# Low parts of the smaller weight tiles of the attention stages subtracted by GpSimd in place of VectorE, in a four-layer transformer kernel on one core

## What is computed

```python
# block 1, per layer                     # block 2, per layer
x = x + 0.5*swiglu(rmsnorm(x), ...)      h = adaln(rms_norm(x), shift1, scale1)
h = rmsnorm(x)                           proj = h @ w_in            # q, k, v, gates
q, k, v, ..., gates = h @ w_in           y_a = swa_attention(...)  @ w_o_swa
y_a = forgetting_attention(...)          y_b = moba_attention(...) @ w_o_moba
y_b = stick_breaking_attention(...)      mixed = sigmoid(gate_a)*y_a + sigmoid(gate_b)*y_b
y_c = dsa_attention(...)  # top-k mask   x = x + gt1 * (mixed @ w_out)
merged = sum(sigmoid(gates)*(y @ w_up))  h = adaln(rms_norm(x), shift2, scale2)
x = x + merged @ w_out                   x = x + gt2 * (relu(h @ w_up)**2 @ w_down)
x = x + 0.5*swiglu(rmsnorm(x), ...)
```

## Time and profile before

| what | value |
|---|---|
| median of 3 runs | 2033.84 us (2031.59 to 2033.9) |
| the profiled execution: its time, its span | 2032.25 us, 2030.6 us |
| granted TensorE clock, mean over the span | 0.996 |
| busy PE, share of the span | 1960.0 us, 97% |
| busy DVE | 1526.7 us, 75%, 2637 instructions |
| busy ACT | 1031.0 us, 51% |
| busy POOL | 44.9 us, 2%, 80 instructions |
| the chain that ended last | PE 82%, DVE 9%, ACT 6%, issue 3%, DMA 1% |

### The profile page before, as it was taken

One profiled execution on the slowest core, in us unless ns is written; L12 is line 12 of the kernel. 1 busy time (PEld: TensorE's weight loads), 2 busy tenths in 40 slices (PEclk: granted clock), 3 DMA queues, 4 the chain that ended last, 5 costly groups with the idle time before them and its releaser, 6 DMA issues.

```text
span 2030.6 us, 32702 instructions
## 1 busy us (share of the span) xinstructions
PE 1960.0 (97%) x11980; PEld 1718.1 (85%) x11980; DVE 1526.7 (75%) x2637; ACT 1031.0 (51%) x1582; POOL 44.9 (2%) x80
## 2 busy tenths in 40 slices
PE   7999999999999999999899999999999999999998
PEld 6888898988888888899888888888788888887887
DVE  7887567579888987657678887785767778667766
ACT  5445545654446444545565445566444455555443
POOL 0000000000000000000000000000000000000000
PEclk9999999999999999999999999999999999999999
DMA  7874543257774876453246774441455544233553
GB/s 298 293 283 172 190 156 131 88 180 280 277 268 153 287 281 215 167 186 125 94 169 247 282 250 150 170 149 71 145 186 186 186 179 173 95 125 135 186 186 135
DMA packets 77286, 382.18 MB, mean 188 GB/s; under 512 B 9296, under 2 KB 9472, under 8 KB 55936
## 3 DMA queue, kind: packets, MB, share of 16 engines
q1 hardware_dynamic: 67392, 329.78, 44.9%
q0 software_dynamic: 9792, 51.00, 7.6%
HBM read 379.65 MB, written 1.10 MB: 188 GB/s over the span
## 4 chain that ended last, share of the span: by engine, by line
PE 82%; DVE 9%; ACT 6%; issue 3%; DMA 1%; SPq 0%; DVEq 0%; ACTq 0%
PE psum L674 21%; PE psum L585 15%; PE psum L586 15%; PE psum L587 15%; PE psum L677 11%; DVE weights_low_a L1446 2%; ACT weights_high_a L1069 1%; PE psum L883 1%; ACT x_normed L1077 1%; PE psum L821 1%; PE psum L812 1%; PE psum L910 1%; PE psum L911 1%; PE psum L909 1%; DMA raw_a<-in_w_ffn_a_a 1%
## 5 line engine op out<-in xcount | busy, mean ns | idle before, releaser
L674 PE MATMUL psum<-h_high_low,weights_high_a 128*128 128x512 f32 x1840 | 654.7, 398 | 5.4 <-DVE h_high_low L1491 3.3
L1446 DVE TENSOR_TENSOR weights_low_a<-raw_a,weights_high_a 128x2048 fp32r<-128x2048 f32 (+1 forms) x232 | 459.8, 1983 | 123.2 <-ACT weights_high_a L1069 121.2
L677 PE MATMUL psum<-h_high_low,weights_low_a 128*128 128x256 f32 x1840 | 514.2, 279 | 0.0
L674 PEld LDWEIGHTS psum<-h_high_low,weights_high_a 128*128 128x128 f32 x1840 | 345.3, 188 | 92.5 <-issue 5.3
L1069 ACT ACTIVATE weights_high_a<-raw_a 128x2048 fp32r<-128x2048 f32 (+1 forms) x232 | 386.0, 1664 | 65.1 <-PE psum L587 61.4
L677 PEld LDWEIGHTS psum<-h_high_low,weights_low_a 128*128 128x128 f32 x1840 | 346.7, 188 | 6.6 <-issue 1.0
L1446 DVE TENSOR_TENSOR weights_low_b<-raw_b,weights_high_b 128x1024 fp32r<-128x1024 f32 x224 | 273.3, 1220 | 54.5 <-ACT weights_high_b L1069 54.0
L1069 ACT ACTIVATE weights_high_b<-raw_b 128x1024 fp32r<-128x1024 f32 x224 | 235.4, 1052 | 104.6 <-PE psum L587 104.6
L1139 ACT ACTIVATE up_low_products<-psum 128x512 f32<-128x512 f32 (+1 forms) x146 | 74.1, 507 | 391.7 <-PE psum L677 391.6
L585 PE MATMUL psum<-weights_high_b,gated_high 128*128 128x512 f32 x608 | 241.8, 398 | 4.6 <-DVE gated_low L1575 2.8
L587 PE MATMUL psum<-weights_high_b,gated_low 128*128 128x512 f32 x608 | 241.3, 397 | 0.0
(11 more groups left out here) (300 smaller groups left out, 3165.9 us busy)
## 6 DMA issues: line engine op xcount, KB each, us to landing
ada_weights<-in_w_ada POOLq DMA_DIRECT2D x64, 768.0 KB, 5.9
raw_a<-in_w_ffn_a_a SPq DMA_DIRECT2D x44, 1024.0 KB, 7.3
raw_a<-in_w_ffn_b_a SPq DMA_DIRECT2D x44, 1024.0 KB, 7.4
raw_a<-in_w_ffn_a SPq DMA_DIRECT2D x64, 512.0 KB, 4.4
raw_b<-in_w_ffn_b SPq DMA_DIRECT2D x64, 512.0 KB, 3.3
raw_a<-in_w_proj_a SPq DMA_DIRECT2D x28, 1024.0 KB, 5.5
raw_a<-in_w_gate_a SPq DMA_DIRECT2D x26, 1024.0 KB, 4.8
raw_b<-in_w_ffn_a_b SPq DMA_DIRECT2D x44, 512.0 KB, 3.9
```

The costliest lines, as they stand in the source:

```text
L674: pe.matmul(ps[:, bank, :], whi[0][:, p, c:c + P], hboth[:, k, :, :].rearrange("p a b -> p (a b)"), start=k == 0, stop=False, skip_group_c ...
L677: last_mm = pe.matmul(ps[:, bank, SEQ:2 * SEQ], wlo[0][:, p, c:c + P], hhi[:, k, :], start=False, stop=k == KD - 1, skip_group_check=True)
L1446: dve.tensor_tensor(wlo[kind][:, p, 0:width], raw[kind][:, p, 0:width], whi[kind][:, p, 0:width].bitcast(F32), ALU.subtract).then_inc(lo_r ...
```

## The change

In the attention stages the low parts of the "b" tiles are subtracted by GpSimd. DVE no longer does them there: 8 tiles per layer in block 1 (slots `FF1+9` to `FF1+16`) and 5 in block 2 (slots 7 to 12, of which slot 11 has no "b" tile), 26 in all. GpSimd waits for the low part of the slot before (so that `lo_ready[1]` still counts in order) and for ACT's high part. In `merge`, DVE waits for GpSimd's last tile before it goes on with its own. The "a" tiles and all splits outside the attention stages stay as they are.

```diff
+            def low_b_ready(l, blk, n):
+                slots = SL[blk]
+                return l * parts_before(slots, 1, len(slots)) + lo_before(blk, 1) + parts_before(slots, 1, n + 1) + 2
+
+            def split_low_b(l, blk, first, end):
+
+                for n in range(first, end):
+                    p, width = n % 2, SL[blk][n][1] * P
+                    if not width:
+                        continue
+                    pool.wait_ge(lo_ready[1], low_b_ready(l, blk, n - 1))
+                    pool.wait_ge(now().hi_ready[1], parts_before(SL[blk], 1, n + 1))
+                    pool.tensor_tensor(wlo[1][:, p, 0:width], raw[1][:, p, 0:width],
+                                       whi[1][:, p, 0:width].bitcast(F32), ALU.subtract).then_inc(lo_ready[1], 1)
...
+                if blk == 2:
+                    split_low_b(l, 2, 7, 13)
                 if blk == 1:
 
+                    split_low_b(l, 1, FF1 + 9, FF1 + 17)
                     pool.wait_ge(now().scale_ready, 2 * NT + 1)
...
-                    if g is not None and g % 3 == 0:
-                        split_low(l, blk, 1, n0 + g // 3 + 1)
...
                 split_low(l, blk, 0, n0 + 1)
+                dve.wait_ge(lo_ready[1], l * parts_before(SL[blk], 1, len(SL[blk])) + lo_before(blk, 1)
+                            + parts_before(SL[blk], 1, n0 + 1) + 2)
```

## The result

| | before | after |
|---|---|---|
| median of 4 runs each, us | 2033.13 | 2044.64 |
| profiled span, us | 2030.6 | 2042.2 |

The ratio is 1.0056, with an interval of 1.0044 to 1.0069: the change makes the kernel slower by about 11.5 us. The forecast was 2037.6 us with a range up to 2042.5. The sign had been given the larger chance (slower 0.41, faster 0.25); the size lies outside the range.

The account below looks back on a forecast made before the run. PE, busy 97%, bounds the kernel, so only its waits and slow stretches count. The places sum to +2.8 us, twice +5.6, less 1.85 for the clock: +3.8, 2037.6 us on the median, range 2026.5 to 2042.5.

Parts of the forecast that it names:

- The hold itself: A DVE instruction with two SBUF inputs stands still for the rest of a running GpSimd subtraction; forecast's chance 0.60.
- A: Start of the block-1 stage: stick-breaking sums held until near 302.4, cost 0.8 us instead of a 0.93 gain.
- B: Block 1, at 309.44: L1696 waits 1.96 us for GpSimd; less 0.42 slack, PE's gate tile loses 1.5 us.
- GpSimd's price: Length of one GpSimd subtraction of a 128x1024 tile, taken as 2.29 us.
- D: Start of the block-2 stage: squares at 1325.04 wait 1.9 us for GpSimd; cost 0 to 1.9, taken as 0.4.
- C: Top-k stretch of block 1: a split of 1.13 us leaves DVE's chain; gain taken as 1.0 us.
- The wait of 3.73 us: PE's idle time before about 357 in block 1's top-k stretch; forecast to shrink to about 2.7 us.
- E: Block 2, near 1348: GpSimd may take its turn before DVE's pair at L1882; 0 to 2.25 us, taken as 1.1.
- F: Block 2, two-element TENSOR_SCALAR L1725 at 1342.42 in the changed kernel; the forecast had no term for it.
- The clock term: Low PE clock from 357 to 362 in block 1: a shorter wait avoids it in one layer, 1.85 us back.
- The hold is dearer: Rival, chance 0.12: GpSimd takes 3 us or more, or always its turns at E; 2041 to 2046 us.

Follow-up runs that it names:

- the kernel in which GpSimd does nothing: Changed kernel with all its semaphores kept but the 26 GpSimd subtractions left out, so products take what lies in the buffers; 2030.16 us, ratio 0.9988.
- that of slot 9: Kernel before with only slot 9 of block 2 moved to GpSimd, one tile per layer; 2041.23 us, ratio 1.0043.
- the kernel of slot 8: Kernel before with only slot 8 of block 2 moved to GpSimd, one tile per layer; one run took 2033.74 us.
- second trace of before: The kernel before, unchanged, profiled once more; 2033.38 us.
- the kernel that copies: Changed kernel, but GpSimd copies the raw tile into the low part in place of subtracting; 2033.48 us.

## Why the prediction was wrong

*The hold itself* was right: a full stop for the whole instruction. "It decides as soon as DVE's instructions at A and B keep their lengths": they did not.

*GpSimd's price* was 2.29 for 2.40 us. The estimate from the Trainium skill, "GPSIMD Engine Reference", § Performance versus the Vector engine (4497 ns, halved to 2.25 us), is 0.15 too low. The tiles were in time, and the new waits cost nothing (the kernel in which GpSimd does nothing).

*A, B and D* were +0.8, +1.5 and +0.4; they measured +0.46, +1.68 and +0.5. Their sum is 0.1 us off per pair of layers, and part of that is luck. At A the rotation was all but over when GpSimd came, and the instruction held was a small copy with one input, a kind that the forecast did not count. At B the forecast saw PE lose time only at its gate tile; 0.99 us of the loss is already there at 314.82, where PE waits for the turned probabilities, and 0.68 at the gate tile of 323.31.

*C* was "1.0, since the chain goes on through DVE on both sides of it and 3.73 us of idle PE are there to be taken". It gave 0.66. The trace shows why. DVE had no idle time from 340 to 352 in the kernel before; with the split gone it gets to the next scores before PE has them ready, and waits:

```profile
349.50 0.29 DVE L1717 CUSTOM_DVE_ANT_0 scores<-psum,constants 128x128 f32<-128x128 f32 x1 [0.33 <-PE psum L844]
```

Another 0.16 us goes at a row maximum that GpSimd holds (0.33 us at 347.54 for 0.17); 0.66, 0.33 and 0.16 make up the 1.13 of the chain. In the kernel in which GpSimd does nothing DVE's wait is 0.50. The wait of 3.73 us could not shrink by this split: the chain ends it through DVE's work from 350.8 on (a split of 2.19 us, top-k rounds, row maxima) and ACT's exponentials, and PE's work before it, at 350.72, is released by DVE's row maximum of L1701. Both of its ends lie behind the removed split and move together. It stayed 3.7 us in all thirteen traces; what shrank was the wait before both, from 0.92 us before 350.72 to 0.25 before 352.96.

*The step that failed first is E*: "I take the middle, 1.1". It measured 2.05 both times, near the upper end of 2.25, and again 2.09 and 2.08 alone. GpSimd waits for the running instruction and then always got its turn, in the changed kernel and in that of slot 9. Over both layers 1.9 us.

*F was missing*, 1.4 us over both layers. The prediction counted as exposed only "DVE instructions that read two tensors in SBUF". A TENSOR_SCALAR of two elements, from which ACT's sink exponentials and the score chain hang, is held as well. The row that showed the hold was one for a TENSOR_SCALAR; the list of exposed instructions should have started from it.

*The clock term had the wrong sign.* It took 1.85 us back on the ground that C shortens the wait of 3.73 us. The wait did not shorten, and behind it the changed kernel got -0.60 and +0.78, +0.2 in sum: the low clock was half as long as before in the first layer and twice as long in the second. Kernels with block 1 untouched moved by -0.62 to +0.89 in the same stretch, so neither value can be laid to the change. Where the change did touch the clock, at E, it cost 1.5 us in one layer; the forecast had nothing there. Together 3.6 us, the largest part of the error. Of the signs named ahead, PE's wait before 304.66 grew from 1.06 to 1.51 us and a new one of 0.43 appeared at 323.31, as said; "the wait of 3.73 us at 357 down to 2.7" did not come.

E +1.9, F +1.4, clock +3.6, C +0.7, A, B and D -0.1, and 0.8 of the kernel's own start make 8.3; with the small steps of -0.5, that is 7.8 between +3.8 and the 11.6 of the profile. The rival *The hold is dearer* is the one that came true, by its second condition ("its turns at E are always taken"): its 2041 to 2046 us hold the result, A, B, D and E come to 9.4 us in its +8 to +12, and its chance of 0.12 was too small. That it hits the time as well is in part luck: it takes +8 to +12 for the whole difference, and what it leaves out (C -1.3, F +1.4, clock +1.8, start +0.8, small steps -0.5) comes to only +2.2. The chances don't add up either: half of 0.60, 0.12 and 0.03 make 0.45 for slower, not 0.41.

What stays open: why the clock fell behind E in the first layer and not in the second of the changed kernel, though PE's waits were 1.31 and 0.87 us in one and 1.33 and 0.87 in the other, and in both layers with slot 9 alone.

## What to carry to other kernels

Before work goes from VectorE to GpSimd, list what VectorE does in the microseconds after GpSimd's release. Where GpSimd reads SBUF, every instruction with two SBUF inputs and every small SBUF copy or TENSOR_SCALAR tried here was held for the rest of GpSimd's instruction; the copies and TENSOR_SCALARs were held by a GpSimd that only writes, too. Even one of two elements costs TensorE time if it stands on TensorE's path. Move only the tiles whose window is free of them, or cut GpSimd's instruction into pieces; and look first whether the work can't wait in VectorE's own queue until VectorE idles. Where one collision is taken away, VectorE is earlier, so the next has to be looked at anew. Count an instruction that leaves a chain only up to the next place where the chain waits for another engine, and look whether it lies ahead of the wait or inside it: ahead of it, both ends of the wait move.

## What the runs showed of the hardware

- DVE's waiting for GpSimd shows as busy time, not as idle time before an instruction: 1531.7 us busy for less work than the 1526.7 of before. POOL's waiting shows in the same way (2.91 for 2.40 us).
- GpSimd's preparation of a transfer holds DVE as well, and the kernel before has it: its first trace shows no case, its second one. The cast begins at 582.65 and ends at 583.33, 0.09 us behind POOL, 0.68 us in place of 0.29. In the kernel of slot 8 the same cast took up to 1.17 us. First POOL, then DVE, second trace of before:

```profile
581.80 1.44 POOL L525 DMA_DIRECT2D modulation_sums<-modulation_scratch  x1 [4.92 <-DMA modulation_scratch<-modulation_rows]
```

```profile
582.65 0.68 DVE L1570 CAST gated_high<-gated 128x256 fp32r<-128x256 f32 x1
```

- GpSimd took 2.40 us for a subtraction of 128x1024, 0.95 for filling the same tile and 1.04 for copying it.
- Not held beside a running GpSimd subtraction: MAX8, MATCH_REPLACE8 and the score reductions that read PSUM (0.42 us at 1341.95, the same as before).
- Between thirteen traces the low clock in the top-k stretch came in two lengths only: the mean over 350 to 366 was 0.79 or 0.89, and over 970 to 990 0.83 or 0.91, whichever kernel it was. PE's own wait before it was 3.7 us in all thirteen.
- A stretch at 1.2 GHz of the shorter kind, 1.5 us at PE, also appeared in the second layer of block 2 behind no new wait, in the kernel that copies and in that of slot 8 (0.86 over 1765 to 1777, where before has 1.00).
- A low clock cost nothing where PE was soon to wait for another engine anyway. The kernel before ran at 0.50 from 1642.0 to 1645.4; in the kernel in which GpSimd does nothing the clock stayed up there, PE was 1.55 us earlier for it, and lost all of that by 1650 in a wait for DVE's `x_normed`.
